# The second search of a PEER router over 80 rank pairs instead of 256, and twice the gathered dot products ahead of the last stage

## The reference, cut to what matters

```python
s = jnp.einsum('phcd,hckd->phck', qy, sub_keys)          # 8 heads, 2 sides, 128 keys
top_s, top_i = lax.top_k(s, PEER_TOPK)                   # 16 of each side, sorted
cand_s = top_s[:, :, 0, :, None] + top_s[:, :, 1, None, :]
cand_i = top_i[:, :, 0, :, None] * N_KEYS + top_i[:, :, 1, None, :]
best_s, best_j = lax.top_k(cand_s.reshape(PEER_BLOCK, PEER_HEADS, PEER_TOPK * PEER_TOPK), PEER_TOPK)
experts = jnp.take_along_axis(cand_i.reshape(...), best_j, axis=-1)
gate = jax.nn.softmax(best_s, axis=-1)
u = expert_u[experts]
v = expert_v[experts]
act = jax.nn.gelu(jnp.einsum('pd,phkd->phk', xb, u), approximate=False)
return jnp.einsum('phk,phkd->pd', gate * act, v)
```

## Time and the profile before

| | |
|---|---|
| median of 3 runs | 3586.72 us (3586.11 to 3587.93) |
| span of the profiled execution | 3586.0 us |
| TensorE busy | 3358.9 us, 94% of the span |
| VectorE busy | 2581.0 us, 72% |
| ScalarE busy | 1175.5 us, 33% |
| GpSimd busy | 849.9 us, 24% |
| tile stage | about 1191 to 1598 us |
| block stage | about 1598 to 1998 us |
| rest | about 1998 to 2486 us |

### The profile page before, as it was taken

How to read it: one execution, slowest core, us unless ns; L and a number is a source line. 1 busy time by engine, 2 the same in 40 slices (tenths; PEclk the granted TensorE clock), 3 DMA queues, 4 the chain that set the end, 5 groups by cost and what they waited for, 6 DMA issues and landing times. The chain is left out here.

```text
span 3586.0 us, 53735 instructions
## 1 busy us (share of the span) xinstructions
PE 3358.9 (94%) x18867; PEld 3063.5 (85%) x18867; DVE 2581.0 (72%) x4943; ACT 1175.5 (33%) x2011; POOL 849.9 (24%) x904
## 2 busy tenths in 40 slices
PE   5997999899799799999999999998899999999998
PEld 4997999878688799999999999998688888888886
DVE  6435777454688889988988666761777777777777
ACT  3003556442322222237777322222222222222220
POOL 1000111111000011111111566651233333333331
PEclk8998999999899899999999999999999999999999
DMA  6622222154111244546676899984989898989896
GB/s 255 221 99 93 79 90 90 50 185 130 61 47 35 90 145 142 160 145 237 233 268 245 305 342 344 347 314 136 280 284 292 283 294 282 294 281 295 280 294 242
DMA packets 420834, 743.17 MB, mean 207 GB/s; under 512 B 224368, under 2 KB 275744, under 8 KB 416032
## 3 DMA queue, kind: packets, MB, share of 16 engines
q0 software_dynamic: 98624, 369.14, 29.9%
q1 hardware_dynamic: 318624, 318.99, 28.2%
q10 hardware_dynamic: 3392, 52.47, 3.5%
HBM read 607.30 MB, written 133.19 MB: 206 GB/s over the span
## 5 line engine op out<-in xcount | busy, mean ns | idle before, releaser
L466 PE MATMUL apab<-h2hi,auhib 128*128 128x384 f32 x2048 | 706.5, 345 | 43.4 <-DVEq L60 39.0
L467 PE MATMUL apab<-h2lo,auhib 128*128 128x384 f32 x2048 | 688.2, 336 | 0.0
L468 PE MATMUL apab<-h2hi,aulob 128*128 128x384 f32 x2048 | 688.0, 336 | 0.0
L1661 POOL DMA_INDIRECT vrow<-in_expert_v,fw_now x256 | 312.4, 1220 | 716.7 <-DVE acc L1687 699.1
L466 PEld LDWEIGHTS apab<-h2hi,auhib 128*128 128x128 f32 x2048 | 387.7, 189 | 49.1 <-DVEq L60 43.7
L467 PEld LDWEIGHTS apab<-h2lo,auhib 128*128 128x128 f32 x2048 | 387.7, 189 | 0.0
L468 PEld LDWEIGHTS apab<-h2hi,aulob 128*128 128x128 f32 x2048 | 386.9, 189 | 0.0
L1745 ACT ACTIVATE ageb<-apab 128x384 f32<-128x384 f32 x256 | 125.8, 492 | 659.6 <-PE apab L468 640.8
L1687 DVE SCALAR_TENSOR_TENSOR acc<-vrow,fw_share,acc 128x1024 f32<-128x1024 f32 x256 | 327.1, 1278 | 0.9 <-DVE ga L2236 0.5
L2306 PE MATMUL evo<-vhi,Hhi 128*128 128x512 f32 x768 | 300.4, 391 | 12.8 <-DVE acc L2262 8.8
L1710 POOL DMA_DIRECT2D aurb<-in_expert_u x128 | 71.6, 560 | 997.5 <-DVEq L60 697.4
(11 more groups left out here) (319 smaller groups left out, 7412.7 us busy)
## 6 DMA issues: line engine op xcount, KB each, us to landing
aurb<-in_expert_u POOLq DMA_DIRECT2D x128, 512.0 KB, 4.6
vraw<-in_expert_v SPq DMA_DIRECT2D x128, 512.0 KB, 4.0
ahead_dram<-ageb SPq DMA_DIRECT2D x256, 192.0 KB, 4.7
gates_dram<-arena ACTq DMA_DIRECT2D x12, 4096.0 KB, 12.0
ga<-ahead_dram SPq DMA_DIRECT2D x128, 384.0 KB, 5.9
gr<-gates_dram SPq DMA_DIRECT2D x128, 384.0 KB, 7.6
late<-in_w_ada SPq DMA_DIRECT2D x48, 512.0 KB, 5.9
gw<-in_w_in POOLq DMA_DIRECT2D x8, 1408.0 KB, 8.5
```

The lines of the kernel that those rows point to most:

```text
L466: pe.matmul(out, lhi, rhi, start=(k == 0), stop=False)
L467: pe.matmul(out, lhi, rlo, start=False, stop=False)
L468: return pe.matmul(out, llo, rhi, start=False, stop=(k == n - 1))
L1661: pool.indirect_dma_start(self.ring[i], None, table, bass.IndirectOffsetOnAxis(ap=self.now[:, h, i:i + 1], axis=0)).then_inc(self.row_in[i ...
```

## The change

- **Search.** The candidates are 80 sums per head instead of 256: rank 0 of the first list with all 16 of the second, ranks 1 to 7 with the first 8, and ranks 8 to 15 with rank 0. They are made in three additions. MAX8, FIND_INDEX8 and MATCH_REPLACE8 read 80 elements instead of 256. The two ranks are worked out from the position in eight small operations instead of three.
- **Tile stage.** Eight dots per dense tile instead of four, in pairs at the same four places.
- **Block stage.** Four U rows per block instead of two, and eight dots instead of four. A group of four tokens has 12 matmuls of U rows instead of 6.
- **Rest.** What is left is 32 U rows, of which the first 28 have four dots each.

The number of U rows, dots, gathers and matmuls in the whole phase stays the same. The diff, without the lines that only shift an index:

```diff
-NBEST = TOPK * TOPK
+ROWS_CUT = 8
+NBEST = TOPK + (ROWS_CUT - 1) * ROWS_CUT + ROWS_CUT
...
-ROWS_BLOCK = 2
-ITEMS_BEST = DT * RING
-ITEMS_GATE = TD // 64 * RING
+ROWS_BLOCK = 4
+BLOCK_BATCHES = 2
+ITEMS_BEST = DT * 2 * RING
+ITEMS_GATE = TD // 64 * BLOCK_BATCHES * RING
...
+                for n in range(RING):
+                    gather(n)
+                for d in range(DT):
+                    row, n = (FEW + d) * R + 2, d * 2 * RING + RING
+                    for j in range(3):
+                        load(row + j, j % 2)
+                    for j in range(3):
+                        gather(n + 2 * j)
+                        gather(n + 2 * j + 1)
+                        load(row + 3 + j, (3 + j) % 2)
+                    gather(n + 6)
+                    gather(n + 7)
...
+                        for c in range(BLOCK_BATCHES):
+                            batch = b * BLOCK_BATCHES + (ITEMS_BEST // RING + c)
+                            few.choose(pool, batch, c, batch * RING)
+                            for i in range(RING):
+                                few.gather(pool, table, batch, c, i)
+                                if i % 2 == 0:
+                                    j = 2 * c + i // 2
+                                    load(b * ROWS_BLOCK + (ROW_GATE + 2 + j), j % 2)
...
                             if k == 1:
-                                A.cut_high(act, r + 1, 1 - j, (b + (ROW_GATE // 2 + j)) * 16 + 16)
-                            if k == 4:
+                                A.cut_high(act, r + 1, 1 - j % 2, (r + 1) // 2 * 16 + 16)
+                            if k == PER // 2:
                                 A.gelu(act, r, 0)
...
-                    def dot(i):
+                    def dots(i):
                         if not sparse:
-                            few.dot_row(dve, (t + (-FEW)) * RING + i, i)
+                            for n in range(2 * i, 2 * i + 2):
+                                few.dot_row(dve, (t + (-FEW)) * (2 * RING) + n, n % RING)
...
-                    link(dve.tensor_single_scalar(code[:, 0], bf, 4, ALU.logical_shift_right))
-                    link(dve.tensor_single_scalar(code[:, 1], bf, 15, ALU.bitwise_and))
-                    link(dve.tensor_copy(rank[:, :, :], code[:, :, :]))
+                    link(dve.tensor_single_scalar(code, bf, 3, ALU.logical_shift_right))
+                    link.together([dve.tensor_copy(found[:, 0], code), dve.tensor_copy(found[:, 1], bf)])
+                    link(dve.tensor_scalar(rank[:, 0], found[:, 0], -1.0, 0.0, ALU.add, ALU.max))
+                    link(dve.scalar_tensor_tensor(rank[:, 0], found[:, 1], -float(NBEST - TOPK), rank[:, 0], ALU.add, ALU.max))
+                    link(dve.scalar_tensor_tensor(found[:, 0], rank[:, 0], 1.0, rank[:, 0], ALU.min, ALU.add))
+                    link(dve.scalar_tensor_tensor(rank[:, 1], found[:, 0], -float(ROWS_CUT), found[:, 1], ALU.mult, ALU.add))
+                    link(dve.tensor_scalar(rank[:, 1], rank[:, 1], 0.0, None, ALU.max))
...
-                            if gi % RING == RING - 1:
-                                i = gi // RING
-                                few.dot_row(dve, b * RING + (ITEMS_BEST + i), i)
+                            if gi % 2:
+                                n = gi // 2
+                                few.dot_row(dve, b * (BLOCK_BATCHES * RING) + (ITEMS_BEST + n), n % RING)
                             j, k = divmod(gi, PER)
-                            if k == 4:
-                                A.cut_low(link, b * 2 + (ROW_GATE + j + 1), 1 - j)
+                            if k == PER // 2:
+                                A.cut_low(link, b * ROWS_BLOCK + (ROW_GATE + j + 1), 1 - j % 2)
```

48 lines of the change are left out of this document (21 added, 27 removed).

## The result

The changed kernel takes 3596.12 us (median of 9 runs, 3594.37 to 3599.73) against 3587.58 us for the kernel before (9 runs, 3581.73 to 3590.54): ratio 1.0025, 95% interval 1.0016 to 1.0035. It is slower by a quarter of a per cent, just over the 0.2% that the prediction named as what can be told from no change (the interval's lower end is under it). The forecast was 3590 us, within 3574 to 3603; it had given "within 0.2%" a chance of 0.45 and "slower" 0.36, and what came is on the slower side.

A forecast was written before the change was run, and what follows sets the result against it. The prediction took TensorE's own work to bound the kernel, so only its waits could change: 13.9 + 4.5 - 5.8 - 9.2 = +3.4 us on the 3586.0 span, 3589.4, with 0.7 for the median 3590; range 3574 to 3603.

The forecast's parts named there:

- rival 2: Whole kernel, the forecast itself: stall in the tiles about paid for by blocks and rest, 3590 us, chance 0.55.
- rivals 1, 3 and 4: 1: tile chain fits, 3571.7, chance 0.15; 3: block cuts late, 3600 to 3614, 0.2; 4: seam stores held, 3612, 0.05.
- Tile stage, +13.9: Six dense tiles: cut(2) to cut(4) grows, so TensorE waits 2.31 us more per tile at the row behind cut(4).
- Clock, +4.5: Dense tiles: granted clock drops behind three of the six long waits, 1.5 us each; bounds 0 and 9.
- Blocks, -5.8: Block stage: the 24 waits of 0.29 us go, 0.24 net each; the 1.79 at the seams stays.
- slack of 0.22: Blocks: group 3 can start at 5.74 us and is due at 5.96; cost behind the cut taken as 0.
- Rest, -9.2: Rest: the rows behind row 99 go, and their 9.2 us of waits with them; bounds -5 to -13.
- What the first 28 lose remains: Rest: the first 28 rows were taken to lose what they lose in the kernel before.
- rival 5: Rest: rows with gathers keep losing from the first on, -9.2 becomes about 0, time 3599; chance 0.05.
- Rival 4: Block seams: stores held behind the gate store; 2 us excess at each of 11 seams is +22, 3612; chance 0.05.
- slack of 14.6: Block seams: GELU store's buffer wanted again 14.6 us later; ScalarE's queue can bear about a group more, to 17.5.

The follow-up runs named there:

- tiles8: Kernel before with the 80-candidate search and eight dots per dense tile, blocks as before: 3607.71 us, ratio 1.0047.
- one_moved: Changed kernel with three instead of four dots between cut(2) and cut(4), still eight per dense tile: 3585.08 us, ratio 0.9994.
- spread: Changed kernel with its eight dots per dense tile dealt out 1, 1, 2, 1, 1, 2, two between cut(2) and cut(4): 3573.04 us, ratio 0.9956.
- search80: Kernel before with only the 80-candidate search and its index code: 3592.22 us, ratio 1.0005.
- spread_first: spread with two gathers of the first rest batch put ahead of a row's load in GpSimd's queue: 3570.67 us, ratio 0.9951.
- spread_late: spread with the last gate store moved from the seam to behind the 30th row of the rest: 3568.06 us, ratio 0.9949.
- spread_best: spread with the edits of spread_first and spread_late, and ScalarE's next-block last row ahead of the GELU at seams: 3551.00 us, ratio 0.9902; again 3553.09.
- before_best: Kernel before with three edits: next block's last row ahead of the GELU, late last gate store, two early gathers: 3575.59 us, ratio 0.9964.

## Why the prediction was right or wrong

**The time came out 6.1 us above the 3590 forecast, within its range.** The mechanism named (rival 2) is the one that happened in tiles and blocks, and rivals 1, 3 and 4 did not: no chain that fits, no cut that comes late in the blocks, no seam held by a store. The third term, the rest, failed.

- **Tile stage, +13.9: right.** Six waits of 2.34 to 2.36 at the place named, out of a chain worked out as 24.13 and measured as 24.18. Six waits of 0.19 to 0.20 at cut(3), which I had not listed, add 1.2. tiles8, one_moved and spread show that the chain is the cause, dot by dot.
- **Clock, +4.5 (bounds 0 and 9): four drops instead of three**, 6.1 us. What decides whether a wait of 2.34 brings one is not settled: equal waits gave 0.72 and 1.00, and those of 1.2 never a drop. That half of them was assumed was a guess between the bounds.
- **Blocks, -5.8: right**, -6.4. The 24 waits of 0.29 went, the seams stayed at 1.80, and the slack of 0.22 behind the cut held: one wait of 0.2 in 48. Of the difference 0.27 is the seam of 2.07: I had put 1.79 at all 11 seams, and 11 of those with 24 of 0.29 are 26.7 us, not the 24.9 of the earlier trace rows.
- **Rest, -9.2: this is the step that failed.** The profiled execution gave back 2.1. Since such losses scatter by up to 4 us, more profiles say it better: the two kernels with the old blocks and 46 rows with gathers (before, search80) lost 23.4 on the mean, the three with the rest code of the change (after, one_moved, spread) 18.5, which is -4.9. "What the first 28 lose remains" was wrong: I took the first 28 rows from the kernel before, where 15 of them lose nothing, and assumed that these would still lose nothing behind a different block. At the 28th row the loss was 13.2 and 13.0 in the first two and 19.0, 16.3 and 17.1 in the other three. The lead is made in the last block: the cut, and with it the load that stands ahead of the first gathers, comes 2.6 us nearer to the end, the gathers come 3.3 us ahead instead of 5.9, beside the gate store, and the lead is gone after 3 rows instead of 12 to 17. spread_first, which puts two of them back, loses 13.0 at its 28th row, as the kernel before does; that the two numbers are so near is partly luck, as its first step is smaller (4.2 against 6.9) and its flat part shorter. A smaller part of the miss: the 9.2 hold the 2.2 us that the kernel before loses behind the last row with gathers, and the changed kernel loses 1.3 there too.
- My bounds (-5 to -13) held the runs with the same rest code only in part: against 22.4 they gave -2.1, -3.8 and -5.8.
- The price of rival 5, "the rest keeps losing", was the nearest to what came; it had 0.05, which was too little, since nothing in my working spoke for the lead being the same.
- **Rival 4 was argued down with the wrong row.** The median of 4.9 us in the earlier trace rows holds no store issued beside a gate store: at each of the 11 seams of the kernel before, the store issued 0.99 to 1.27 us behind the gate store has no landing in the trace, and the next one comes 11.8 to 12.1 us behind it. What held was the other half of the argument, the slack of 14.6.

The sum by measured terms: 14.1 (six waits) + 1.2 (cut(3)) + 6.1 (clock), less 6 x 0.16 that was there before, is 20.4 of the 20.5; with -6.4, -2.1 and -1.2 outside the three stages that gives the 10.8 between the spans (rounded terms).

The prediction cited the Trainium skill, page "DMA: Bandwidth & Descriptors", section "Queues, rings and completion order": a transfer's semaphore write lands only after every earlier write of its DMA engine. The traces agree. At the end of the blocks of the changed kernel the small store issued behind the GELU of 2209.49 frees its buffer at 2224.73, 15.2 us later, and with the gate store gone (spread_late) the same buffer is free without a wait within 8.3 us. In the two profiles of spread_best ScalarE waits for such a store at each of the 11 seams, and where the gate store's landing is on record, the buffer comes free just behind it: landed at 1991.94, free at 1992.22; 2086.63 and 2087.49; with the late store 2437.00 and 2437.22; in all twelve cases 0.2 to 0.9 us. The DMA engines were full meanwhile (share 0.98 from 2208 to 2225 in the changed kernel), and no run separates how much of the time is due to that. TensorE pays nothing for it in the blocks. In the changed kernel no seam shows a wait for a store: the slack of 14.6 us that I had worked out was enough.

## What to carry to other kernels

Work added to an engine with room on average can still cost its full length if it stands in the chain between two cuts that another engine releases; look for the slack of that chain, not of the engine, and put such work where the engine waits for someone else. When rows are moved out of a stage that lives on a lead, ask what builds the lead: counting its first rows as they were is only right if the handing-over stage is left as it was. Where the profile names one engine for a wait and two fill the same tile, see which of them ended last. And the same edit of a chain is worth what of the chain is exposed: 3.27 us of it showed 0.29 in one kernel and 1.32 in the other.

## What the runs showed of the hardware

- Equal waits of TensorE (2.34 us, at the same place of each tile) were followed by a granted clock of 0.72 over the next 6 us four times and by 1.00 twice, in the same order in tiles8. The length of the wait alone does not decide it: in the rest of before_best one of 2.08 was followed by 0.72, in that of search80 one of 3.23 by 1.00. Six waits of 1.2 us were followed by 1.00 each time, and so were the seams of 1.3 to 1.8 us. Going from 2.34 to 1.2 gave back 12.7 us in six tiles, nearly twice the waits' own 6.8.
- A 192 KB store issued 0.6 to 2.0 us behind a 4096 KB store of another queue freed its buffer only when that one had landed: 0.2 to 0.9 us behind the landing in twelve of twelve cases of spread_best and its repeat, and 12 to 15 us behind its own issue. Moved behind the rows with gathers, the big store cost TensorE 1.1 us in four profiles and 2.1 in one (before_best).
- The same rest code lost 16.6 to 20.3 us in three kernels, and 6.8 and 10.8 in two profiles of one kernel: a stage in which the DMA engines are at 0.9 is the part of this kernel that repeats worst.
